# Moving the activations of the up stages by 64 bytes, to the place in SBUF that the other stages use

## What is computed

```python
# block 1
h = rmsnorm(x, g_attn);  proj = h @ w_in            # 2048 x 6152
x = x + mixed @ w_out                                # 2048 x 2048
h2 = rmsnorm(x, g_mlp)
u = relu(h2 @ w_up)                                  # 2048 x 8192   "up"
x = rmsnorm(x + (u * u) @ w_down, g_final)           # 8192 x 2048   "down"
# block 2
proj = rmsnorm(x) @ w_in_2;  h = x + mix @ w_out_2
hn = rmsnorm(h, ffn_norm_g)
q = hn @ peer_w_query                                # 2048 x 2048   "queries"
gates over 16384 experts from q and the sub-keys
y = (gate * gelu(hn @ peer_u.T)) @ peer_v            # 16384 experts, up and down
```

## Time and profile before

| | |
|---|---|
| median of 3 runs | 3208.42 us (3207.24 to 3208.45) |
| the profiled execution | 3207.3 us |
| its span, first to last instruction | 3205.3 us |
| TensorE busy | 3187.0 us, 99% of the span |
| VectorE / ScalarE / GpSimd busy | 2030.2 / 1447.6 / 496.9 us |
| granted TensorE clock | 0.999 of full speed |
| HBM read | 606.31 MB |

### The profile page before, as it was taken

One profiled execution on the slowest core, in us unless ns is written; L12 is line 12 of the kernel. 1 busy time (PEld: TensorE's weight loads), 2 busy tenths in 40 slices (PEclk: granted clock), 3 DMA queues, 4 the chain that ended last, 5 costly groups with the idle time before them and its releaser, 6 DMA issues.

```text
span 3205.3 us, 48201 instructions
## 1 busy us (share of the span) xinstructions
PE 3187.0 (99%) x19975; PEld 2864.7 (89%) x19975; DVE 2030.2 (63%) x1837; ACT 1447.6 (45%) x1271; POOL 496.9 (16%) x418
## 2 busy tenths in 40 slices
PE   8999999999999999999999999999999999999999
PEld 7888899999999888888989999999999888888887
DVE  5455665555555667766466888999974555555554
ACT  5454453334343464464444444555543443343343
POOL 0000000000000002226300001988840000000000
PEclk9999999999999999999999999999999999999999
DMA  7444465555555443343256565677676666566563
GB/s 288 162 161 163 173 225 185 193 186 192 188 187 192 171 164 131 126 161 115 93 184 221 199 215 215 233 247 243 241 262 248 237 255 247 225 249 249 227 269 119
DMA packets 129572, 644.18 MB, mean 201 GB/s; under 512 B 12672, under 2 KB 45840, under 8 KB 60304
## 3 DMA queue, kind: packets, MB, share of 16 engines
q1 hardware_dynamic: 95792, 623.03, 53.5%
q10 hardware_dynamic: 33632, 18.99, 1.9%
HBM read 606.31 MB, written 35.66 MB: 200 GB/s over the span
## 4 chain that ended last, share of the span: by engine, by line
PE 97%; DVE 1%; ACT 1%; DMA 0%; SPq 0%; issue 0%; DVEq 0%; ACTq 0%
PE pj L313 12%; PE pj L314 12%; PE pj L315 12%; PE pj L289 7%; PE pj L290 7%; PE pj L291 7%; PE pj L1786 4%; PE pj L1788 4%; PE pj L904 4%; PE pj L1787 4%; PE pj L906 4%; PE pj L905 4%; PE pm L290 2%; PE pt L290 2%; PE pt L291 2%; PE pm L291 2%
## 5 line engine op out<-in xcount | busy, mean ns | idle before, releaser
L271 ACT ACTIVATE hi<-raw 128x2048 fp32r<-128x2048 f32 x534 | 1023.8, 1917 | 1374.1 <-PE pj L315 653.2
L278 DVE TENSOR_TENSOR lo<-raw,hi 128x2048 fp32r<-128x2048 f32 x400 | 918.2, 2296 | 679.8 <-ACT hi L271 679.2
L313 PE MATMUL pj<-xh_up,hi 128*128 128x256 f32 x3328 | 925.1, 278 | 0.0
L314 PE MATMUL pj<-xl_up,hi 128*128 128x256 f32 x3328 | 924.1, 278 | 0.0
L315 PE MATMUL pj<-xh_up,lo 128*128 128x256 f32 x3328 | 924.1, 278 | 0.0
L315 PEld LDWEIGHTS pj<-xh_up,lo 128*128 128x128 f32 x3328 | 628.8, 189 | 0.0
L314 PEld LDWEIGHTS pj<-xl_up,hi 128*128 128x128 f32 x3328 | 625.1, 188 | 0.6
L313 PEld LDWEIGHTS pj<-xh_up,hi 128*128 128x128 f32 x3328 | 624.9, 188 | 0.5
L278 DVE TENSOR_TENSOR lo_in<-raw,hi 128x2048 fp32r<-128x2048 f32 x134 | 308.3, 2301 | 267.6 <-ACT hi L271 266.8
L2509 POOL TENSOR_SCALAR hotA<-cst,slotT 128x128 fp32r<-128x128 f32 x256 | 338.1, 1336 | 460.9 <-ACT slotT L2347 424.5
L1786 PE MATMUL pj<-hi,xh_tok 128*128 128x512 f32 x576 | 231.2, 401 | 0.0
(11 more groups left out here) (412 smaller groups left out, 4239.0 us busy)
## 6 DMA issues: line engine op xcount, KB each, us to landing
raw<-w_peer SPq DMA_DIRECT2D x256, 1024.0 KB, 6.3
raw<-w_mlp SPq DMA_DIRECT2D x128, 1024.0 KB, 4.8
raw<-w_in SPq DMA_DIRECT2D x102, 1024.0 KB, 4.9
raw<-w_out SPq DMA_DIRECT2D x32, 1024.0 KB, 4.9
raw<-w_q SPq DMA_DIRECT2D x16, 1024.0 KB, 5.2
act_scratch<-hidU SPq DMA_DIRECT2D x32, 512.0 KB, 3.0
gates_scratch<-stage ACTq DMA_DIRECT2D x8, 2048.0 KB, 17.7
hidV<-act_scratch SPq DMA_DIRECT2D x32, 512.0 KB, 3.7
```

What stands on the lines that cost most here:

```text
L271: nc.scalar.activation(hi[:, j, :], raw[:, j, :], ACT.Copy).then_inc(hi_ready, 1)
L278: nc.vector.tensor_tensor(low(q)[:, j, :], raw[:, j, :], hi[:, j, :].bitcast(F32), ALU.subtract).then_inc(lo_ready, 1)
L313: nc.tensor.matmul(o, hi[:, j, cols], xh_up[:, k0 + k, :], start=clears, stop=False, skip_group_check=True)
L314: nc.tensor.matmul(o, hi[:, j, cols], xl_up[:, k0 + k, :], start=False, stop=False, skip_group_check=True)
```

## The change

The two sets become one, `xh` and `xl`, at the place that the token stages had (64 bytes past the cursor, 256 bytes from the weights). The up stages and the queries and experts read it too. `xl` stands straight behind `xh`; what lies behind both moves down by 512 bytes, so that its address modulo 512 stays. `dn`, a small array of block 2, moves from the space of the tail weights into the region that its neighbours use. No instruction is added, removed or moved on any engine: the count and order on each of the five are those of before.

```diff
-TOK_SHIFT = 64
+X_SHIFT = 64
...
-        xh_up = sb("xh_up", [P, KT, TT * P], F32R)
-        xh_tok = sb("xh_tok", [P, KT, TT * P], F32R, at=at_x + TOK_SHIFT)
-        cursor[0] += 512
-        at_xl = cursor[0]
-        xl_up = sb("xl_up", [P, KT, TT * P], F32R)
-        xl_tok = sb("xl_tok", [P, KT, TT * P], F32R, at=at_xl + TOK_SHIFT)
-        cursor[0] += 512
+        xh = sb("xh", [P, KT, TT * P], F32R, at=at_x + X_SHIFT)
+        xl = sb("xl", [P, KT, TT * P], F32R, at=at_x + 4 * KT * TT * P + X_SHIFT)
+        cursor[0] += 8 * KT * TT * P + 512
...
-                    nc.tensor.matmul(o, hi[:, j, cols], xh_up[:, k0 + k, :], start=clears, stop=False, skip_group_check=True)
-                    nc.tensor.matmul(o, hi[:, j, cols], xl_up[:, k0 + k, :], start=False, stop=False, skip_group_check=True)
-                    mm = nc.tensor.matmul(o, lo[:, j, cols], xh_up[:, k0 + k, :], start=False, stop=end and b % 2 == 1, skip_group_check=True)
+                    nc.tensor.matmul(o, hi[:, j, cols], xh[:, k0 + k, :], start=clears, stop=False, skip_group_check=True)
+                    nc.tensor.matmul(o, hi[:, j, cols], xl[:, k0 + k, :], start=False, stop=False, skip_group_check=True)
+                    mm = nc.tensor.matmul(o, lo[:, j, cols], xh[:, k0 + k, :], start=False, stop=end and b % 2 == 1, skip_group_check=True)
...
-        def stationary(n):
-            return (xh_up, xl_up) if n in (2, 5) else (xh_tok, xl_tok)
...
-        dn = sb("dn", [P, 3, TT, H], at=at_tail + 4 * KT * 16)
+        dn = z("dn", [P, 3, TT, H])
```

More of the change, by code:

```diff
@@ L505, in lift_pe @@
             tr.then_inc(tp, 1)
-        def stationary(n):
-            return (xh_up, xl_up) if n in (2, 5) else (xh_tok, xl_tok)
         def lift_act(act, n, b, gain, free=None):
-            xh, _ = stationary(n)
             act.wait_ge(tp, 4 * n + b - 3)
@@ L520, in lift_dve @@
         def lift_dve(dve, n, b, gain):
-            xh, xl = stationary(n)
             dve.wait_ge(tp_h, 4 * n + b + 1)
@@ L532, in first_lift_act @@
             for k in range(4 * b, 4 * b + 4):
-                ins = nc.scalar.activation(xh_tok[:, k, :], xT[:, k, :], ACT.Copy, scale=small[:, S_GATTN + k:S_GATTN + k + 1])
+                ins = nc.scalar.activation(xh[:, k, :], xT[:, k, :], ACT.Copy, scale=small[:, S_GATTN + k:S_GATTN + k + 1])
             ins.then_inc(tp_h, 1)
@@ L538, in first_lift_dve @@
             for k in range(4 * b, 4 * b + 4):
-                ins = nc.vector.scalar_tensor_tensor(xl_tok[:, k, :], xT[:, k, :], small[:, S_GATTN + k:S_GATTN + k + 1],
-                                                     xh_tok[:, k, :].bitcast(F32), ALU.mult, ALU.subtract)
+                ins = nc.vector.scalar_tensor_tensor(xl[:, k, :], xT[:, k, :], small[:, S_GATTN + k:S_GATTN + k + 1],
+                                                     xh[:, k, :].bitcast(F32), ALU.mult, ALU.subtract)
             ins.then_inc(tp_l, 1)
@@ L592, in parts_pe @@
                         tok = slice(t * P, (t + 1) * P)
-                        nc.tensor.matmul(pair[:, t, :], xh_tok[:, 4 * j + k, tok], hi[:, j, cols], start=j == 0 and k == 0, stop=False)
-                        nc.tensor.matmul(pair[:, t, :], xh_tok[:, 4 * j + k, tok], lo_in[:, j, cols], start=False, stop=False)
-                        mm = nc.tensor.matmul(pair[:, t, :], xl_tok[:, 4 * j + k, tok], hi[:, j, cols], start=False, stop=False)
+                        nc.tensor.matmul(pair[:, t, :], xh[:, 4 * j + k, tok], hi[:, j, cols], start=j == 0 and k == 0, stop=False)
+                        nc.tensor.matmul(pair[:, t, :], xh[:, 4 * j + k, tok], lo_in[:, j, cols], start=False, stop=False)
+                        mm = nc.tensor.matmul(pair[:, t, :], xl[:, 4 * j + k, tok], hi[:, j, cols], start=False, stop=False)
             mm.then_inc(pe_used, 1)
@@ L621, in tail_pe @@
             for k in range(KT):
-                nc.tensor.matmul(pm[0:2 * cols, 0, 0:TT * P], wtail_s[:, k, 0:2 * cols], xh_tok[:, k, :],
+                nc.tensor.matmul(pm[0:2 * cols, 0, 0:TT * P], wtail_s[:, k, 0:2 * cols], xh[:, k, :],
                                  start=k == 0, stop=False, skip_group_check=True)
-                mm = nc.tensor.matmul(pm[0:cols, 0, 0:TT * P], wtail_s[:, k, 0:cols], xl_tok[:, k, :],
+                mm = nc.tensor.matmul(pm[0:cols, 0, 0:TT * P], wtail_s[:, k, 0:cols], xl[:, k, :],
                                       start=False, stop=k == KT - 1, skip_group_check=True)
@@ L903, in dense @@
                         begin, end = first and kk == 0, last and kk == 3
-                        nc.tensor.matmul(pair[:, t, :], xh_tok[:, k0 + kk, tok], hi[:, j, cols], start=begin, stop=False)
-                        nc.tensor.matmul(pair[:, t, :], xh_tok[:, k0 + kk, tok], lo_in[:, j, cols], start=False, stop=False)
-                        mm = nc.tensor.matmul(pair[:, t, :], xl_tok[:, k0 + kk, tok], hi[:, j, cols], start=False, stop=end)
+                        nc.tensor.matmul(pair[:, t, :], xh[:, k0 + kk, tok], hi[:, j, cols], start=begin, stop=False)
+                        nc.tensor.matmul(pair[:, t, :], xh[:, k0 + kk, tok], lo_in[:, j, cols], start=False, stop=False)
+                        mm = nc.tensor.matmul(pair[:, t, :], xl[:, k0 + kk, tok], hi[:, j, cols], start=False, stop=end)
                         if kk == 3 and t == 0 and last:
```

## The result

The changed kernel takes 3261.84 us (median, 3261.21 to 3262.4), the kernel before 3208.12 us in the runs beside it. The ratio is 1.0168, with a 95% interval from 1.0156 to 1.0181: **53.7 us slower**, where I had forecast 12.6 us faster. The profiled execution has a span of 3260.4 us, 55.1 us more than before.

A forecast was written before the change was run, and what follows sets the result against it. TensorE was taken to bound the kernel; 12.6 us gained in the MLP up stage and 0 elsewhere gave 3208.4 - 12.6 = 3195.8 us, range 3193.5 to 3230.

The forecast's parts named there:

- What bounds the kernel: Whole kernel: TensorE, busy 3187.0 of 3205.3 us; a quicker or slower TensorE moves the end by just that much.
- What costs nothing: Token and down stages, `dn` and moved arrays: 0; the 256 matmuls of L2299: at most 1.1 us.
- Two steady paces at 192, chosen at restarts: Up stages: matmuls start every 113.3 or 117.8 ns, 4.45 ns apart; the two reads' relation at a restart decides.
- The 12.6 us that I saw in the MLP: MLP up stage: 59 slow chunks, 2832 matmuls, each 4.45 ns quicker after the change: 12.6 us gained.
- the choice between the bounds: Up stages at 256: between 12.6 us gained and 31.9 us lost, took the gain, as 256-byte down stages run quick.
- The bound above: MLP, queries and experts: at worst all up stages in the slow pace, 30.8 + 1.1 = 31.9 us lost.
- Slow everywhere: Rival, up stages: 256 bytes gives the slow pace; MLP stays slow, 149 other chunks join: 3240 us, chance 0.10.
- The rival "turned round": Up stages: MLP turns quick after 8 chunks, queries and experts slow: +19.9 us, 3228 us; chance 0.19 whole, 0.12 in part.
- the partial cases: Queries and experts: only part of 144 chunks turns slow, 3204.6 or 3214.9 us; chance 0.12, about 0.05 within no change.
- the sum for "same": Whole kernel: chance of a time within 0.2% (6.4 us) of no change, 0.16 + 0.04 = 0.20.
- The rival "nothing": Up stages: pace hangs on start and form, not on 64 bytes; MLP slow, experts quick, 3208.4 us, chance 0.16.

The follow-up runs named there:

- restart1: Kernel before, with one 128-wide identity transpose ahead of each MLP up super-block from the second on and one behind the row broadcast: 3202.91 us, ratio 0.9985.
- all_64: Kernel before, with all of SBUF from raw to the activations, coefficients included, 64 bytes further on, up stages still 192 bytes from the weights: 3216.69 us.
- restart_1_3: restart1 with three transposes instead of one ahead of the super-blocks of odd parity: 3201.29 us, ratio 0.998 against the kernel before.
- coef_320_64: Kernel before, with the down stages' coefficients moved from 0 and 256 bytes to places where moving minus stationary is 192 and 448: 3233.04 us.

## Why the prediction was wrong

**What bounds the kernel: right.** TensorE has no idle time in these stages, and each ns of pace went into the end: 55.1 us more busy time, 55.1 us more span.

**What costs nothing: right.** The token stages, `dn`, and the arrays behind. For L2299 I had up to 1.1 us, it was 1.2. That its matmuls, whose distance did not change, would be drawn into the pace of their neighbours was in that bound, not in my reasons.

**Two steady paces at 192, chosen at restarts: right, but not the whole.** restart1 turned eight super-blocks of the same chunks from 117.8 to 113.3 ns, and all_64 turned 45 chunks of the queries and experts the other way. The 12.6 us that I saw in the MLP are there; restart_1_3 fetched 6.3 of them net of its breaks. But coef_320_64 changed the pace with no restart. That it is the stand of two reads to each other which a restart sets was my idea, and no run shows it.

**The step that failed** is the choice between the bounds: "If 64 bytes shift that relation, the up stage at 256 is quick in it." It took the relation of two streams with 512 moving columns over to a stage with 256, where no row had shown it. Of the distances tried, the best ones of the two forms are opposite. With 256 columns 0 and 256 are the worst of those tried, and 192 and 448 the best. With 512 columns 0 and 256 are the good ones: the token stages lost 1.4 ns each at 320, the down stages 6.7 ns (30.7 us over 4608) at 192 and 448. The two forms differ in more than the columns, as the weights are the moving operand in one and the stationary one in the other; no run separates the two.

**The bound above failed too.** I had 31.9 us, "both stages in the slow pace", since I knew two paces and took the slower for the worst. 120.0 ns is a third. Slow everywhere had the right place and sign, with a term that was mis-sized: 4.45 ns for 149 chunks instead of 6.67 ns for 149 and 2.2 ns for 59, so 3240 where 3262 came. The rows of before bound what the streams do at a distance that they have, not at a new one; the token stages' first steps at a restart, 233 ns for twice the columns, were not a ceiling either.

**The rival "turned round"** did not occur: at 256 no chunk is quick after any restart or any down stage. At 128 and 160 the MLP and the experts hold different paces, but it is the MLP that is slower again. Only with `xl` alone at 256 does the MLP hold the quicker pace and a part of the queries and experts the slower, and both are slow beside 113.3 ns.

**Smaller slips.** The super-block of the earlier trace rows, 482.86 to 505.48 us, is the third, not the second. Of the partial cases 0.05 were to end within the bound of no change, and the sum for "same" took 0.04. Neither changes the forecast.

**The rival "nothing"** fell. A view moved by 64 bytes, with every instruction the same, costs 1.7%. The Trainium skill ("SBUF — State Buffer", "Who interferes with whom") has TensorE's two read ports as independent; what I drew from that, that no distance matters, did not come out, and the measurement decides. It also says that TensorE never waits on anyone: where the other engines and the transfers stood still, the pace was 120.0 ns all the same, so the loss is no sign of waiting on one of them. What inside the chip ties the pace to the distance no run shows.

Open are also what divides restarts at 192 into the quick and the slow (one transpose cures about every second super-block, two cure none, three cure five of the six that one did not and spoil one that it did), why it is every second super-block with coef_320_64 and with restart1, and why the up stages and the stages with 512 columns want opposite distances.

## What to carry to other kernels

In a stream of matmuls without idle time, place the moving and the stationary operand on purpose, and scan the distance per form of matmul, by the distance of starts rather than the rows' durations. What is best for one form can be worst for another, as here for 512 moving columns of weights and 256 of activations. Bound such a change by a run of the new place alone, since the trace of before holds no ceiling for it; and look for two paces of one instruction in a trace, because a short break at the right place may buy back the quick one; here that gave 6.3 us of 3208, with places found by trial.

## What was not expected of the hardware

- The pace of a 128x256 fp32r matmul, all else equal, went from 113.3 to 120.0 ns by the distance of its operands alone; 0 and 256 bytes gave the same, as did 192 and 448.
- One and the same stream kept either of two paces, 4.4 ns apart, over hundreds of us and through down stages of 21.8 us, until a break of one transpose, or other coefficients in the down stage, changed it.
- 32 bytes off the good distance cost 31 to 40 us of 3208 (160 and 224 against 192).
- The cost isn't a matmul's own: with only `xl` at 256, half of the loss lay in the steps behind the two matmuls whose operands had stayed at 192.
